# Adding up the squares of the features on VectorE before the product with ones, in the norms of a hybrid decoder trunk

## What is computed

```python
def rmsnorm(x, g):
    xf = x.astype(jnp.float32)
    y = xf * lax.rsqrt(jnp.mean(xf * xf, axis=-1, keepdims=True) + EPS)
    return (y * g.astype(jnp.float32)).astype(x.dtype)

for l in range(DEPTH):
    ...
    h = rmsnorm(x, norm1_g[l]) * (1.0 + sc1) + sh1
    x = x + g1 * hybrid_mixer(h, positions, rel_bias, w_in[l], ...)
    h = rmsnorm(x, norm2_g[l]) * (1.0 + sc2) + sh2
    x = x + g2 * peer_ffn(h, peer_w_q[l], ...)
return rmsnorm(x, final_g)
```

## Time and profile before

| | |
|---|---|
| time, median of 3 runs | 2254.84 us (2251.26 to 2256.5) |
| the profiled execution's own time | 2254.05 us |
| its span, first to last instruction | 2252.3 us |
| TensorE busy, matmuls | 2140.1 us (95%) |
| VectorE busy | 1547.3 us (69%) |
| ScalarE busy | 1226.8 us (54%) |
| GpSimd busy | 440.0 us (20%) |
| mean granted TensorE clock | 0.979 of 2.4 GHz |

### The profile page before, as it was taken

The page is one execution under the profiler, slowest core; times in us unless marked ns, Lnnn a source line. Parts: engine busy times, 40 slices in busy tenths (PEclk is TensorE's granted clock), DMA queues, the critical chain, the costliest instruction groups (busy, mean ns, idle before and its releaser), DMA issues.

```text
span 2252.3 us, 39908 instructions
## 1 busy us (share of the span) xinstructions
PE 2140.1 (95%) x13732; PEld 1947.7 (86%) x13732; DVE 1547.3 (69%) x3026; ACT 1226.8 (54%) x2330; POOL 440.0 (20%) x184
## 2 busy tenths in 40 slices
PE   5799999999999999999999989999999999999997
PEld 4688789999999978888878978999999997888886
DVE  7688458991678867777758945899168885555555
ACT  8623434555788844444443343454578884554553
POOL 0000056898000000000000005689800000000000
PEclk9799999999999999999999999999999999999999
DMA  7723244545444457777763323445544444555552
GB/s 261 277 85 122 95 133 140 169 165 189 131 132 147 133 174 262 261 261 262 258 208 117 122 75 133 140 168 168 187 132 138 142 135 140 192 195 194 190 193 102
DMA packets 103475, 378.80 MB, mean 168 GB/s; under 512 B 11488, under 2 KB 11872, under 8 KB 102880
## 3 DMA queue, kind: packets, MB, share of 16 engines
q1 hardware_dynamic: 102672, 373.74, 49.4%
q10 hardware_dynamic: 720, 4.00, 0.5%
HBM read 375.46 MB, written 2.23 MB: 168 GB/s over the span
## 4 chain that ended last, share of the span: by engine, by line
PE 72%; issue 9%; POOL 7%; DVE 5%; DMA 3%; ACT 2%; SPq 0%; POOLq 0%; DVEq 0%; ACTq 0%
PE bank L1751 29%; PE bank L1654 8%; PE bank L1655 8%; PE bank L1656 8%; POOL split_lo L477 7%; PE bank L1718 5%; PE bank L1391 4%; DMA ring<-stream 2%; PE bank L1403 1%; PE bank L1642 1%; PE bank L1353 1%; DMA ada_ring<-stream 1%; DVE grid L855 1%; ACT split_hi L685 1%; PE bank L1427 1%
## 5 line engine op out<-in xcount | busy, mean ns | idle before, releaser
L1654 PE MATMUL bank<-h_hi,split_hi 128*128 128x256 f32 x2304 | 668.7, 290 | 25.2 <-POOL split_lo L477 11.1
L1655 PE MATMUL bank<-h_lo,split_hi 128*128 128x256 f32 x2304 | 653.9, 284 | 0.0
L1656 PE MATMUL bank<-h_hi,split_lo 128*128 128x256 f32 x2304 | 653.8, 284 | 0.0
L1251 DVE TENSOR_TENSOR split_lo<-ring,split_hi 128x1024 fp32r<-128x1024 f32 x248 | 303.8, 1225 | 251.3 <-ACT w_hi L773 251.3
L1654 PEld LDWEIGHTS bank<-h_hi,split_hi 128*128 128x128 f32 x2304 | 443.7, 193 | 32.0 <-POOL split_lo L477 16.8
L477 POOL TENSOR_TENSOR split_lo<-ring,split_hi 128x1024 fp32r<-128x1024 f32 x168 | 433.2, 2603 | 175.4 <-ACT split_hi L685 175.2
L772 ACT ACTIVATE split_hi<-ring 128x1024 fp32r<-128x1024 f32 x248 | 263.2, 1061 | 361.6 <-PE bank L1751 361.6
L1655 PEld LDWEIGHTS bank<-h_lo,split_hi 128*128 128x128 f32 x2304 | 444.4, 193 | 0.0
L1656 PEld LDWEIGHTS bank<-h_hi,split_lo 128*128 128x128 f32 x2304 | 443.6, 193 | 0.0
L685 ACT ACTIVATE split_hi<-ring 128x1024 fp32r<-128x1024 f32 x296 | 298.6, 1051 | 211.9 <-PE bank L1656 211.8
L1751 PE MATMUL bank<-split_hi,w_hi 128*128 128x512 f32 x1024 | 316.9, 391 | 0.0
(11 more groups left out here) (273 smaller groups left out, 2546.2 us busy)
## 6 DMA issues: line engine op xcount, KB each, us to landing
ring<-stream SPq DMA_DIRECT2D x658, 512.0 KB, 3.4
ada_ring<-stream SPq DMA_DIRECT2D x48, 512.0 KB, 4.3
spill<-tables ACTq DMA_DIRECT2D x1, 1152.0 KB, 4.3
tables<-spill ACTq DMA_DIRECT2D x1, 1152.0 KB, 7.1
xT<-x_in SPq DMA_DIRECT2D x1, 1024.0 KB, 9.6
s5raw<-s5w ACTq DMA_DIRECT2D x2, 512.0 KB, 5.6
y_out<-hT SPq DMA_DIRECT2D x1, 1024.0 KB, 3.9
KM<-mixc SPq DMA_DIRECT2D x1, 576.0 KB, 7.6
```

What stands on the lines that cost most here:

```text
L1251: v.tensor_tensor(split_lo[:, s, :], ring[:, (late + j) % RING, :], split_hi[:, s, :].bitcast(F32), ALU.subtract)
L1654: mm(dst, hi, x_hi, start=start, stop=False, skip_group_check=not group)
L1655: mm(dst, hi, x_lo, start=False, stop=False, skip_group_check=not group)
L1656: return mm(dst, lo, x_hi, start=False, stop=stop, skip_group_check=not group)
```

## The change

In every norm but the first of layer 0, VectorE adds the eight blocks of squares into block 0 (`add_square`), and TensorE makes one product with ones (`sum_of_squares`) instead of eight. The additions are written between the residual updates: after residual m comes the addition of square m - 1, and the last square after the loop. For m = 0 `add_square` only waits. The additions 1 to 6 are linked; the seventh counts the new semaphore `sq_summed`, for which TensorE waits. `sum_of_squares` has no `free_block`, which moves to the first filler.

```diff
+        sq_summed = sem("sq_summed")
...
+                def add_square(n, m):
+
+                    dve.wait_ge(sq_ready, KT * (n + 1) + m + 1)
+                    if m:
+                        ins = v.tensor_tensor(sq[:, 0, :], sq[:, 0, :], sq[:, m, :], ALU.add)
+                        if m < KT - 1:
+                            link(ins)
+                        else:
+                            ins.then_inc(sq_summed, 1)
+
                 for m in range(KT):
                     v.scalar_tensor_tensor(xT[:, m, :], take(l, f"out{m}"), mod2[:, l, 2 * KT + m:2 * KT + m + 1], xT[:, m, :],
                                            ALU.mult, ALU.add).then_inc(dve_taken, 1)
+                    if m:
+                        add_square(2 * l, m - 1)
+                add_square(2 * l, KT - 1)
...
                     v.scalar_tensor_tensor(xT[:, m, :], bank[:, m, 0:T],
                                            mod2[:, l, 5 * KT + m:5 * KT + m + 1], xT[:, m, :], ALU.mult, ALU.add).then_inc(x_done, 1)
+                    if m:
+                        add_square(2 * l + 1, m - 1)
+                add_square(2 * l + 1, KT - 1)
...
+            def sum_of_squares(n, r):
+
+                pe.wait_ge(sq_summed, n)
+                mm(r, ones, sq[:, 0, :], start=True, stop=True).then_inc(region_filled, 1)
+
             def keep_running(n):
 
-                for _ in range(n):
-                    mm(bank[:, 6, 0:P], ident, ones, start=True, stop=True)
+                for k in range(n):
+                    last = mm(bank[:, 6, 0:P], ident, ones, start=True, stop=True)
+                    if k == 0:
+                        free_block(last)
...
-                sums_of(l, "ss1", sq, KT, 2 * KT * l)
+                if l:
+                    sum_of_squares(2 * l, free_region(l, "ss1"))
+                else:
+                    sums_of(l, "ss1", sq, KT, 0)
                 keep_running(30)
...
-                sums_of(l, "ss2", sq, KT, 2 * KT * l + KT)
+                sum_of_squares(2 * l + 1, free_region(l, "ss2"))
                 keep_running(36)
...
-            for k in range(KT):
-                pe.wait_ge(sq_ready, 2 * KT * DEPTH + k + 1)
-                last = mm(bank[:, 0, 0:T], ones, sq[:, k, :], start=(k == 0), stop=(k == KT - 1))
-            last.then_inc(region_filled, 1)
+            sum_of_squares(2 * DEPTH, bank[:, 0, 0:T])
```

## The result

The changed kernel takes 2260.19 us in the median of 8 runs (2257.31 to 2263.99), the kernel before 2253.82 us in the median of 8 (2251.26 to 2256.5): a ratio of 1.0029, 95% interval 1.0018 to 1.0040, +6.4 us. The forecast was 2262.0, from a sum of +7.2 us. The profiled execution of the changed kernel took 2262.89 us, with a span of 2261.1; that is one of its slower runs, 8.8 us of span above the one of before. All times compared here are of executions at a mean granted clock of 0.97 or more; one execution of a later kernel (three larger additions) took 3482.43 us at 0.564 and is in no ratio.

The account below looks back on a forecast made before the run. Four stretches waiting for a norm were taken as decisive, with VectorE the chain in layer 1's first norm. Terms 3.7, 2.5, clock 0.4 + 0.6, and 0 at the second norms sum to +7.2: 2262.0 us, range 2256.0 to 2267.0.

Parts of the forecast that it names:

- the two places: First norm of layer 1 (B) and closing norm (D), where the forecast put the added time: 3.7 and 2.5 us.
- A0 and A1 gain nothing, since ScalarE's three splits hold the root: Second norms of layers 0 and 1: the root queues behind three weight splits, so fewer products gain 0, twice.
- Rival (1): Second norms of both layers: the products hold the root, so -1.6 us twice, +4.0 in all, 2258.8 us; chance 0.08.
- An addition holds VectorE for 0.46 us, a pair for 0.85: Changed norms: a linked 128x256 addition costs VectorE 0.46 us; alternating with a 0.39 us residual, 0.85 us a pair.
- B +3.7 us through VectorE's phase work: First norm of layer 1: additions and waits for squares delay VectorE's phase work and everything after by 3.7 us.
- D +2.5, and +0.4 for the clock: Closing norm: additions alternating with residuals delay the root 2.5 us; the product at TensorE's low clock adds 0.4.
- B's projections lose 0 to 1.3 us to the clock; +0.6 taken: First projections after layer 1's first norm: a low TensorE clock after idling costs 0 to +1.3 us, middle +0.6.
- A0 and A1's clock, 0 taken with -1.2 to +1.7 in the range: Second norms of both layers: TensorE's low spell may begin earlier or grow; 0 taken, -1.2 to +1.7 us each.
- rival (3): All four changed norms: longer TensorE idle costs clock everywhere, +10.3 us in all, 2265 us; chance 0.14.
- (4): Second norms of both layers: low clock spells come earlier, hidden by VectorE's splitting, -1.1 us each, +5.0, 2260 us; chance 0.09.
- The seventh addition is caught by GpSimd, rival (2): Second norms of both layers: GpSimd blocks the last addition, root 1.4 us late twice, +10 in all, 2265 us; chance 0.07.
- The release of a ring slot that moves to the first filler costs nothing: Second norm: the last output block's slot frees at about 291.3, not 289.1 us; the fetch behind has 10 us of room.

## Why the prediction was right, step by step

The time, the sign and the two places hold. By the steps of the forecast:

- *A0 and A1 gain nothing, since ScalarE's three splits hold the root*: shown. The root is at 3.68 us with one product or eight; put ahead of two splits it moves by 1.36 us with one product and by 0.23 with eight. Rival (1) is out.
- *An addition holds VectorE for 0.46 us, a pair for 0.85*: the same in the profile after.
- *B +3.7 us through VectorE's phase work*: +3.72 to the reciprocal, gone with the additions of B. Its split, by experiment: 2.97 the additions, 0.75 the waits for squares. That the low clock adds nothing at the reciprocal is read from the rows after: the root ends at 1191.41, and VectorE works without a pause until 1194.64.
- *D +2.5, and +0.4 for the clock*: +3.08, of which 0.60 is the clock and 2.48 the rest. The clock's term was low by 0.2: the product starts 0.15 us after the last addition's end, where I had put 0.04, and that addition itself began at 6.27 us after the first residual and not at 6.19. The size was partly luck: in the seven profiles with this wait and no fillers at D the clock fell 2.7 to 4.7 us after TensorE went idle, in the changed kernel's 0.64 us ahead of the product (2249.29 and 2249.93), and the whole product was at the low clock in all seven. At B, with 4.77 us of idle in the run with three additions, the fall came 0.46 us behind the product's start, and it took 0.76 us.
- *B's projections lose 0 to 1.3 us to the clock; +0.6 taken*: this term failed. The clock was at 0.50 from 1188 us on, the fillers took 8.72 us and brought it back, TensorE then stood 1.57 us and not 2.2 or more, and the projections ran at the full clock: 0. In all eight profiles with additions ahead of B's one product the clock fell within 1 us of that product or earlier, and in all eight it was back at the full level before the first projection; in the five with eight products at B it stayed full. What failed is the step from the low clock to the projections: the fillers took it all.
- *A0 and A1's clock, 0 taken with -1.2 to +1.7 in the range*: the profile has +0.9 and +1.2, and I first took that for rival (3). The runs with eight products and with more fillers showed the same steps: the low spell varies by itself. Zero is what the means bear out within their scatter, and at these places rivals (3) and (4) describe chance and no effect of the change that shows.
- *The seventh addition is caught by GpSimd, rival (2)*: it started 0.92 us ahead of GpSimd's first subtraction, 1.0 forecast. Out.
- *The release of a ring slot that moves to the first filler costs nothing*: at A0 the fourth split starts 12.90 us after the last residual (300.75 - 287.85), as before (301.82 - 288.92).

The sum by what was measured is 3.7 + 3.1 + 0 = 6.8 us, against 6.4 of the medians; the forecast's 7.2 had 0.6 too much for the clock at B's projections and 0.2 too little for it at D. That the median came within 2 us of the forecast is finer than either kernel's scatter (5 to 7 us from lowest to highest), and so in part luck. The margin over 0.2% was 2 us, and the interval, which begins at 0.18%, does not quite exclude that the true difference lies below it.

## What to carry to other kernels

To take work off an engine with 95% busy time pays only where that engine's end is what the next one waits for; here it was a queue of ScalarE, VectorE's own phase work, and a table load. An accumulation on the engine which feeds the producer of its operands is paid twice: its time, and the waits that it puts ahead of the next input. Put such a wait behind the last instruction that others wait for, and look at what the idle engine's clock does before the next product.

## What the runs showed of the hardware

The length of a low spell of TensorE's clock behind the second norm was 3.4, 6.8 and 10.2 us in executions of kernels with the same or nearly the same code there, and fillers which left TensorE idle for less than 0.4 us ahead of it did not shorten what it costs (a step of 4.18 us at A1, 3.33 at A0). At D, where TensorE had stood for 5 us, fillers kept the clock at the full level (1.00 in 2244 to 2246 us) and the product's time at 0.70 us in place of 1.19. After TensorE went idle at B or D in the changed kernels, its clock fell 2.7 to 5.2 us later, at a different moment in each execution of the same code (at B 3.76 us in the changed kernel's profile, 5.23 in the one with more fillers). VectorE's scaling of 128x256 took 0.34 us each with GpSimd idle, and 0.84 us each on the mean (6.73 us for eight) where the first 4.4 us lay beside GpSimd's subtractions.
